# Recurrence gates as two 64-row tiles, a square root moved behind four casts, and cache loads issued one by one

## What is computed

```
r = sigmoid(block_diag(xc, wa) + ba);  i = sigmoid(block_diag(xc, wx) + bx)
log_a = -8 * r * softplus(-lambda);    a = exp(log_a)
b = sqrt(-expm1(2 * log_a)) * (i * xc)
h[t] = a[t] * h[t-1] + b[t]
```

## Time and profile before

| what | value |
|---|---|
| runs | 1395.02, 1396.47, 1397.4 us; median 1396.47 |
| the profiled execution | 1396.84 us, its span 1394.9 us |
| mean granted TensorE clock | 0.998 |
| PE, DVE, ACT, POOL busy | 98%, 64%, 47%, 2% of the span |
| moved by DMA | 243.60 MB, mean 175 GB/s |

### The profile page before, as it was taken

One profiled execution on the slowest core, in us unless ns is written; L12 is line 12 of the kernel. 1 busy time (PEld: TensorE's weight loads), 2 busy tenths in 40 slices (PEclk: granted clock), 3 DMA queues, 4 the chain that ended last, 5 costly groups with the idle time before them and its releaser, 6 DMA issues.

```text
span 1394.9 us, 25447 instructions
## 1 busy us (share of the span) xinstructions
PE 1373.7 (98%) x10566; PEld 1357.2 (97%) x10566; DVE 894.8 (64%) x1180; ACT 665.9 (48%) x896; POOL 34.8 (2%) x68
## 2 busy tenths in 40 slices
PE   9999999999999999999999999999999999999996
PEld 8999999999899999999999999999998999999996
DVE  5555568496865885554685555585887568655444
ACT  5444446445444664444474444463544455544433
POOL 0100000000101000000000000000001000000000
PEclk9999999999999999999999999999999999999999
DMA  6654444755555454444445544446455453554441
GB/s 241 203 178 157 152 166 160 258 179 178 203 191 204 159 182 157 173 154 162 167 167 181 179 154 143 166 172 228 167 202 204 162 200 129 181 180 153 171 166 57
DMA packets 39998, 243.60 MB, mean 175 GB/s; under 512 B 4577, under 2 KB 4593, under 8 KB 16369
## 3 DMA queue, kind: packets, MB, share of 16 engines
q1 hardware_dynamic: 33264, 219.00, 45.0%
q0 software_dynamic: 5936, 22.01, 4.3%
q10 hardware_dynamic: 720, 1.47, 0.3%
HBM read 238.97 MB, written 3.50 MB: 174 GB/s over the span
## 4 chain that ended last, share of the span: by engine, by line
PE 91%; DVE 4%; DMA 3%; ACT 1%; issue 1%; DVEq 0%
PE ps L440 29%; PE ps L439 29%; PE ps L441 29%; DMA raw<-in_w_in 2%; DVE wlo L1030 1%; PE ps L527 1%; ACT whi L733 1%; PE ps L638 1%; PE ps L631 1%; PE ps L654 1%; PE ps L599 0%; PE ps L623 0%; DMA raw<-in_ffn_wg 0%; PE ps L471 0%; PE ps L472 0%
## 5 line engine op out<-in xcount | busy, mean ns | idle before, releaser
L1030 DVE TENSOR_TENSOR wlo<-raw,whi 128x1024 fp32r<-128x1024 f32 (+1 forms) x450 | 510.1, 1141 | 320.6 <-ACT whi L733 316.4
L733 ACT CAST whi<-raw 128x1024 fp32r<-128x1024 f32 (+1 forms) x446 | 437.2, 987 | 505.1 <-PE ps L441 382.9
L439 PE MATMUL ps<-xh,whi 128*128 128x288 f32 (+1 forms) x2144 | 635.6, 296 | 4.4 <-DVE wlo L1030 3.2
L440 PE MATMUL ps<-xl,whi 128*128 128x288 f32 (+1 forms) x2144 | 631.4, 294 | 0.0
L441 PE MATMUL ps<-xh,wlo 128*128 128x288 f32 (+1 forms) x2144 | 630.5, 294 | 0.0
L439 PEld LDWEIGHTS ps<-xh,whi 128*128 128x128 f32 x2144 | 404.4, 189 | 6.9 <-ACT pool L964 2.9
L440 PEld LDWEIGHTS ps<-xl,whi 128*128 128x128 f32 x2144 | 406.1, 189 | 0.7
L441 PEld LDWEIGHTS ps<-xh,wlo 128*128 128x128 f32 x2144 | 405.5, 189 | 0.0
L439 PE MATMUL ps<-hh,whi 128*128 128x288 f32 (+1 forms) x1088 | 322.0, 296 | 0.0
L440 PE MATMUL ps<-hl,whi 128*128 128x288 f32 (+1 forms) x1088 | 319.4, 294 | 0.0
L441 PE MATMUL ps<-hh,wlo 128*128 128x288 f32 (+1 forms) x1088 | 319.1, 293 | 0.0
(11 more groups left out here) (191 smaller groups left out, 747.5 us busy)
## 6 DMA issues: line engine op xcount, KB each, us to landing
raw<-in_w_in SPq DMA_DIRECT2D x48, 1024.0 KB, 4.9
raw<-in_ffn_wg SPq DMA_DIRECT2D x43, 1024.0 KB, 4.9
raw<-in_ffn_wu SPq DMA_DIRECT2D x43, 1024.0 KB, 4.9
raw<-in_ffn_wd SPq DMA_DIRECT2D x32, 1024.0 KB, 4.9
raw<-in_ffn_wd SPq DMA_DIRECT2D x16, 768.0 KB, 4.1
raw<-in_w_o SPq DMA_DIRECT2D x8, 1024.0 KB, 4.9
raw<-in_w_k_mem SPq DMA_DIRECT2D x4, 1024.0 KB, 5.5
raw<-in_w_v_mem SPq DMA_DIRECT2D x4, 1024.0 KB, 5.7
```

Source lines behind the costliest of these rows:

```text
L439: mm(out, wh, mh, start=start, stop=False)
L440: mm(out, wh, ml, start=False, stop=False)
L733: s_.copy(whi[:, s, k0:k1, :], raw[:, s, k0:k1, :]).then_inc(hi_ready, 1)
L1030: return v.tensor_tensor(out, full, high.bitcast(F32), sub)
```

## The change

The gate weights of both gates of one 64-row block lie side by side in one 64x128 tile, two such tiles above each other on the partitions: `bd` is [128, 4, 128] in place of [128, 2, 4, 128]. Each matmul reads 64 partitions of weights and of `xc`, and gives one gate on PSUM partitions 0 to 63 and the other on 64 to 127, for one half of the features. The two halves (e = 0, 1) write different banks. There are as many matmuls as before (8 per layer), and twice as many tanhs (16 of 64 partitions), since each bank now feeds `t1` and `t2` on one half of the partitions. The square root is issued behind the four casts of blocks B+2 and B+3, and the cache loads 5, 6, 7 (9 to 11, 13 to 15) of a batch wait for PE's progress as well.

```diff
-        bd = sb("bd", [P, 2, KB, P])
+        bd = sb("bd", [P, KB, P])
...
-                        g.dma_start(bd[e * h:(e + 1) * h, j, :, e * h:(e + 1) * h],
+                        g.dma_start(bd[e * h:(e + 1) * h, :, j * h:(j + 1) * h],
                                     I[w][l].rearrange("(k e) a b -> e a k b", e=2)[e]).then_inc(bd_in, 16)
...
+                def spread(b):
+                    n = plan.at[l]["B"] + (2, 6, 10)[b // BATCH - 1]
+                    return 2 * n + (0, 4, 5, 6)[b % BATCH]
...
                     if b >= BATCH:
                         pool_e.wait_ge(kv_used, l * (2 * NS) + b - BATCH + 1)
+                        if b % BATCH:
+                            pool_e.wait_ge(pe_half, spread(b))
...
-                        for j in range(2):
-                            mm(ps[:, 4 + 2 * k + j, 0:LO], bd[:, j, 2 * r + k, :], xc[:, 2 * r + k, 0:LO],
+                        for e in range(2):
+                            rows = slice(e * P // 2, (e + 1) * P // 2)
+                            mm(ps[:, 4 + 2 * k + e, 0:LO], bd[rows, 2 * r + k, :], xc[rows, 2 * r + k, 0:LO],
                                start=True, stop=True).then_inc(bd_psum, 1)
...
                     for k in range(2):
-                        for j, t in enumerate((t1, t2)):
-                            act.wait_ge(bd_psum, l * 8 + 4 * r + 2 * k + j + 1)
-                            s_.activation(t[:, 2 * r + k, 0:LO], ps[:, 4 + 2 * k + j, 0:LO], ACT.Tanh, scale=0.5,
-                                          bias=der[:, j, 2 * r + k:2 * r + k + 1]).then_inc(bd_tanh, 1)
+                        for e in range(2):
+                            act.wait_ge(bd_psum, l * 8 + 4 * r + 2 * k + e + 1)
+                            own = slice(e * P // 2, (e + 1) * P // 2)
+                            for j, t in enumerate((t1, t2)):
+                                gate = slice(j * P // 2, (j + 1) * P // 2)
+                                half = s_.activation(t[own, 2 * r + k, 0:LO], ps[gate, 4 + 2 * k + e, 0:LO], ACT.Tanh,
+                                                     scale=0.5, bias=der[own, j, 2 * r + k:2 * r + k + 1])
+                            half.then_inc(bd_tanh, 1)
...
                     if i == 0:
                         act.wait_ge(lru_d, l + 1)
-                        s_.activation(t1[:, :, 0:LO], t1[:, :, 0:LO], ACT.Sqrt).then_inc(lru_sqrt, 1)
                     gates(0, i)
...
                     hi(n + 3, 0)
                     hi(n + 3, 1)
+                    if i == 0:
+                        s_.activation(t1[:, :, 0:LO], t1[:, :, 0:LO], ACT.Sqrt).then_inc(lru_sqrt, 1)
```

More of the change, by code:

```diff
@@ L388, in _ @@
             g.memset(junk[:, :], 1.0).then_inc(consts, 1)
-            g.memset(bd[:, :, :, :], 0.0).then_inc(bd_zero, 1)
+            g.memset(bd[:, :, :], 0.0).then_inc(bd_zero, 1)
             pool_e.wait_ge(bd_zero, 1)
@@ L1040, in _ @@
             dve.wait_ge(bd_zero, 1)
-            v.tensor_copy(hh[:, KF - 1, 0:BC], bd[:, 0, 0:2, :].rearrange("p k c -> p (k c)")).then_inc(warm_ready, 1)
+            v.tensor_copy(hh[:, KF - 1, 0:BC], bd[:, 0:2, :].rearrange("p k c -> p (k c)")).then_inc(warm_ready, 1)
             for c in range(PAIRS_D):
```

## The result

The change makes the kernel slower: 1399.68 us median of 8 runs (1396.66 to 1401.68) against 1395.09 for the kernel before, 8 runs beside it. The ratio is 1.003, its 95% interval 1.002 to 1.004. Forecast were 1393.8 us, at most 1396.3, with a chance of 0.06 for slower. The profiled execution took 1400.81 us, its span 1398.9, which is 4.0 more than before.

The account below looks back on a forecast made before the run. PE, busy for 98% of the span, was taken to bound the kernel. Terms of -2.1, -1.8, +1.5 and -0.2 gave -2.6 us on the profiled 1396.84, so 1394.2, or 1393.8 as median; range 1389.8 to 1396.3.

Parts of the forecast that it names:

- the second batch: Cache loads issued one by one lie beside B+10's weight load: 0.75 us lost in each layer, 1.5 in all.
- the sum: Whole kernel: -2.1 - 1.8 + 1.5 - 0.2 = -2.6 us on the profiled 1396.84, giving 1394.2, median 1393.8.
- the second batch costs what the first did: Rival at B+10's load: price 2.9 us in layer 0, 2.0 in layer 1, giving 1397.3; chance 0.08.
- the signs that I had named for being wrong: B+10's load still 4.8 us in layer 0, B+4's 4.9, or gate tanh or `pz` releasing PE.
- Gates as tiles, PE: In `lru_gates`, overlapping halves save 0.75 us per call, calls taking about 1.35 us in place of 2.10.
- Gates, ACT: Eight tanhs take 4.2 us; in the second gate call they put B+2's first cast at 327.62, not 326.56.
- The root: Moved from between B+2's casts, root and table load are free; B+4's load is issued 1.1 us earlier.
- Up to B+6: From the gates to block B+6: 2.1 us gained in layer 0, 1.8 us in layer 1.
- What was to show it: Signs at gates, B+4's load and B+6, plus both waits ahead of L654 (`prompt_values`) longer by 0.75 us.
- First batch: Spread, it thins out around B+6: one cache load, 0.75 us, beside layer 0's B+6 load instead of a backlog.
- `pz`: POOL's clears of `pz`, behind load 11, end at 376.5; DVE wants them at 376.91: free by 0.4 us.
- Start: At kernel start, clearing half as much lets the first matmuls start earlier: 0.2 us gained (0 to 0.5).

Follow-up runs that it names:

- e12: The kernel before with the second half of its clearing put behind POOL's wait for x, so first matmuls start at 2.7 us; ratio 1.0007.
- e7: The kernel before with the square root alone moved; 1393.55 us, ratio 0.9977.
- e16: e7 with 12 unused matmuls of 288 columns added ahead of PE's waits for `prompt_values`; ratio 1.0005 to the kernel before.
- e5: The change with full clearing of `bd` and only the first batch of cache loads (5, 6, 7) spread, later batches four at a time; ratio 0.9994.
- e6: The row tiles alone, with the root and cache loads as in the kernel before and full clearing; ratio 1.002.
- e9: The kernel before with its clearing cut in two halves, one directly behind the other; ratio 0.9996.
- e4: The kernel before with the spreading of the cache loads alone; ratio 1.0029.
- e11: The kernel before with only cache loads 9 to 11 of each layer spread; ratio 1.0035.
- e2: The change with the full clearing (`bd` twice as large, the second half unused); ratio 1.0026 to the kernel before.
- e3: The change without the spreading of the cache loads and with the full clearing, leaving the tiles and the moved root; ratio 0.9988 to the kernel before.
- e1: The change without the spreading of the cache loads (four at a time again), the rest kept; ratio 0.9989 to the kernel before.
- e14: The change with loads 9 to 11 still spread but all issued before B+10's load; ratio 1.0039 to the kernel before.
- e17: The change run once more, unaltered, for a second look; 1401.34 us, ratio 1.0054 to the kernel before.
- e8: The change with 12 unused matmuls of 288 columns ahead of PE's wait for `prompt_values`; ratio 1.0004 to the kernel before.

## Why the prediction was wrong

**The term that failed** is the second batch, "0.75 us lost in each". B+10's load took 4.66 to 5.07 us in layer 0 of the nine profiled kernels with that batch issued together in which it stood in the chain (mean 4.89), and 6.30 to 7.13 in the six with loads 9 to 11 spread as in the change (mean 6.65): 1.8 us more. In layer 1 the means, of those where it stood in the chain, are 6.34 (eight) and 7.28 (five): 0.9 more, where the sum had 0.75; with the loads that stood off the chain they are 6.16 and 7.05, which differ by as much. That is 2.7 in place of 1.5. Two steps made it too small. I counted load 10 alone beside the weights, where load 9's last 2.2 us and load 11's first 1.6 lay beside them as well. And I had bounded the price at 1.4, by halving the 2.9 us that B+6's load of layer 0 took over 4.9. That row needed no halving: the view of 344.8:352.6 of the kernel before, of which the earlier trace rows has another line, shows that this load had only 0.47 MB beside it, about as much as one cache load.

```profile
q0 software_dynamic: 136, 0.47, 14.9%
```

Less the 1.1 us that I charged for its instruction packet, the row gives 1.8, which is what was measured. That it comes out so well is partly luck, because such rows scatter: in e12 B+6's load of layer 0 took 4.85 us beside 0.57 MB and an instruction packet, and in e7 and e16 B+4's took 4.85 and 4.95 with that packet. The nearest thing was the rival "the second batch costs what the first did"; its place was right, its 2.9 us too high for layer 0 as measured, and with what follows below its 1397.3 was still too low. From the Trainium skill (DMA: Bandwidth & Descriptors, Queues, rings and completion order), by which a DMA engine takes turns between queues packet by packet, I had an estimate of 0.8. The rows give 0.9 in layer 1 and about twice that in layer 0, so that this estimate doesn't account for the loss alone; what the rest is no run here shows. None of the signs that I had named for being wrong came (a load of 4.8, a B+4 of 4.9, a tanh or `pz` that releases PE): they asked whether B+10's load would grow at all, and not whether it would grow by too much.

**What the forecast had no term for** is the clock. Falls to half speed between start and end stand in 9 of the 18 traces, and each lies at a wait of PE in stage B. In all traces there are 23 such waits of 1.9 us or more, and 10 of them have a fall that began between 1.1 us before and 1.5 us after PE went on. Of 14 waits of 1.2 to 1.9 us none has one. A fall lasted 3.4 us, once 6.8, and so costs 1.7 us or 3.4. Three of the nine traces (e5, e6, e9) have the second batch issued together: the clock falls in 3 of the 11 traces of that kind and in 6 of the 7 with the batch spread. Over many runs the mean clock says the same: 0.9955 and 0.9947 for the change against 0.9970, which is 2.1 and 3.2 us. So a wait near 2 us can cost more than itself, and spreading made such waits out of the 0.2 and 1.7 us of before. The accounts close within the intervals: e4 lost 4.0 us against the kernel before (2.7 of load, 1.5 of clock), e11 4.9 (2.7 and 1.7), e2 against e3 5.3 (2.7 and 2.8). For the change against e1 they give 2.7 + 2.2 = 4.9 where 5.7 was measured the first time; of the 9 us of the second look 2.7 + 3.4 = 6.1, and the rest is within its wide interval. Of the 5.4 us that e14 lost in the same job the rows give 3.0: -1.5 as e1, 2.3 and 0.2 by B+10's loads, 2.0 by the clock. What the rest is stays open.

**Gates as tiles, PE**: right. 1.25 us per call against the 1.35 predicted; the halves overlap, and 0.2 us go with it.

**Gates, ACT**: eight tanhs took 4.28 against 4.2, right. The first cast of B+2 started 1.5 us later against the gates than before, where 1.06 was predicted, since the first result came only 0.4 us earlier and not 0.75. Behind the first gate call, B+4's load is issued at 21.82 us before and 21.03 after (0.8 earlier, predicted 1.1). It is 19.76 in e7, which has the root alone. So up to this load the root gives 2.06 us and the tiles take 1.27 of them back. I had priced the two only together and did not see that one part works against the other. The difference does not reach `prompt_values`, though: it starts 64.16 and 64.75 us behind the layer's first gate call in e3, which has both, and 63.89 and 64.72 in e7. In e7 B+6's load goes out earlier and takes 8.19 and 8.28 us, beside some 1.55 MB of the first batch. The ratios of e3 and e7 are 1.5 us apart, with intervals that overlap. A loss by the tiles is thus shown with the root at its old place (e6, 2.8 us); beside the moved root neither a loss nor a gain is.

**The root**: right. It and its table load cost nothing at the new place, and `lo(B+2,1)` at 332.96 waited no more for ACT. The way back to tanh stood behind B+4's cast as foreseen, and no gate tanh released PE:

```profile
332.55 1.28 ACT L992 ACT_TABLE_LOAD   x1
333.84 1.26 ACT L992 ACTIVATE pool<-pool 128x1248 f32<-128x1248 f32 x1
340.49 1.05 ACT L741 CAST whi<-raw 128x1024 fp32r<-128x1024 f32 x1 [5.39 <-DMA raw<-in_w_in]
341.55 1.28 ACT L976 ACT_TABLE_LOAD   x1
342.85 0.65 ACT L976 ACTIVATE pool<-ps 128x576 f32<-128x576 f32 x1
```

**Up to B+6**: -1.7 and -1.2 us in the pair, in e17 -1.3 and -1.4, where the sum had -2.1 and -1.8. It was too hopeful by 1.0 in all: 0.3 per layer come from the tanhs, and in layer 0 B+6's load took 6.57 against 6.75 taken, so the size of that term was good (5.98 to 7.13 in e2, e8, e14 and e17).

**What was to show it**: the waits ahead of `prompt_values` did grow, from 0.2 and 1.7 us to 1.82 and 3.78, by two and nearly three times the 0.75. **First batch**: no gain shown (e5 against e3). **`pz`**: cleared by 376.95, wanted at 378.44, free as predicted. **Start**: 0.2 us gained was taken; no gain is shown, and the traces lean to a loss of some 0.6 (see e12).

**The sum** as measured: e1 has -1.5 us for everything but the spreading, the spreading adds about 2.7 by B+10's load and 2.1 to 3.2 by the clock. That makes +3.3 to +4.4, against 4.2 from the first ratio. The second ratio, 7.5 us with 4.7 as its lower end, lies above this. What the remainder is stays open.

## What to carry to other kernels

Price each part of a change alone, even if they come together: here the moved root alone gives 0.9977, and with its two companions it is 1.003, nearly all of it by the spreading (e1 has 0.9989). A transfer that is spread out "to be gentle" on the queues lies beside more of the others' transfers; if a weight load has no slack, ask which data are still on the way in its whole time, and bunch them ahead of it, early enough to have landed. On an engine at 98%, don't let one wait grow towards 2 us: short waits cost themselves, these sometimes cost a stretch at half clock on top, and the mean granted clock over many runs shows it before any single profile does.

## What was not expected of the hardware

- Half clock at waits of PE of 1.97 to 3.78 us, in 10 cases. Thirteen others, of 1.90 to 2.86 us, went without a fall, and what decides between them stays open.
- A 1 MB load of weights (B+10's, layer 0) beside 0.51 to 0.74 MB of another queue's data took 6.3 to 7.2 us in seven traces, in place of 4.9. More megabytes beside it did not mean more time, and B+6's load took 4.85 us beside 0.57 MB in e12.
- An activation of 64 partitions takes as long as one of 128 (8 in 4.28 us, 4 in 2.10), so that gates tiled by rows double ACT's part.
- PE busy without a gap from 9 to 13 us ran at half clock in one execution and at full clock in another, by 18 matmuls against 31. The first entry of full clock came between 8.7 and 13.2 us over the traces.
